# A four-layer transformer and a fifth block on one core: new orders around the sliding-window attention, and mask and maximum in one VectorE instruction

## The reference

```python
scores = jnp.einsum('bnqkgd,bnskd->bnkgqs', qb, kk) * (hd ** -0.5)      # hd = 64, window 128
scores = jnp.where(mask[None, :, None, None], scores, -jnp.inf)          # causal band of 128 keys
sink_col = broadcast(sinks)                                              # one logit for each head
probs = jax.nn.softmax(jnp.concatenate([scores, sink_col], axis=-1), axis=-1)[..., :-1]
out = jnp.einsum('bnkgqs,bnskd->bnqkgd', probs, vv)
```

## Time and profile before

| | |
|---|---|
| median of three runs | 1664.19 us |
| profiled execution | 1669.89 us, of which the span of the core is 1668.1 |
| TensorE matmul / DVE / ScalarE / GpSimd busy | 96% / 73% / 47% / 5% |
| mean granted clock of TensorE | 0.98 |
| first layer's attention, after its first two units | 54.3 to 142.2 us |
| the same in the fourth layer | 1051.0 to 1120.7 us |

### The profile page before, as it was taken

The page is one execution under the profiler, slowest core; times in us unless marked ns, Lnnn a source line. Parts: engine busy times, 40 slices in busy tenths (PEclk is TensorE's granted clock), DMA queues, the critical chain, the costliest instruction groups (busy, mean ns, idle before and its releaser), DMA issues.

```text
span 1668.1 us, 30815 instructions
## 1 busy us (share of the span) xinstructions
PE 1593.7 (96%) x12553; PEld 1504.7 (90%) x12553; DVE 1211.3 (73%) x1619; ACT 792.0 (47%) x1042; POOL 91.1 (5%) x105
## 2 busy tenths in 40 slices
PE   2969999999999999999999999989999999999998
PEld 1848999999989999988899999869999988889998
DVE  6887877778368777765487777958777777676665
ACT  2444433356265334454453334555433467654543
POOL 0131000001000000001100000120000012300000
PEclk8988999999899999999999999999999999999999
DMA  9755787855246888562359785525978745345550
GB/s 391 301 200 204 314 316 293 310 193 199 90 180 250 332 305 317 209 247 101 141 211 362 295 307 221 215 79 201 368 293 319 264 159 166 117 155 194 184 176 26
DMA packets 54219, 383.75 MB, mean 230 GB/s; under 512 B 6256, under 2 KB 6512, under 8 KB 8448
## 3 DMA queue, kind: packets, MB, share of 16 engines
q1 hardware_dynamic: 50400, 363.75, 58.2%
q0 software_dynamic: 3744, 18.94, 3.1%
HBM read 378.47 MB, written 4.19 MB: 229 GB/s over the span
## 4 chain that ended last, share of the span: by engine, by line
PE 85%; DVE 8%; DMA 4%; ACT 1%; issue 1%; POOL 0%; SPq 0%; DVEq 0%; ACTq 0%
PE PS L1855 70%; PE PS L1876 5%; DVE wlo L1329 2%; PE PS L1997 2%; DMA adar<-ada 2%; DMA CST<-cst_in 1%; DVE adar L1347 1%; PE PS L1922 1%; PE PS L1886 1%; DMA raw<-ada 1%; DVE RB L1503 1%; PE PS L2044 1%; DVE SCR L1497 1%; PE PS L1896 1%; PE PS L1976 1%
## 5 line engine op out<-in xcount | busy, mean ns | idle before, releaser
L1855 PE MATMUL PS<-hhi,whi 128*128 128x256 f32 x2496 | 718.7, 288 | 21.8 <-DVE hlo L1537 18.4
L1329 DVE TENSOR_TENSOR wlo<-raw,whi 128x2048 fp32r<-128x2048 f32 x234 | 537.0, 2295 | 247.2 <-ACT whi L931 246.8
L1855 PE MATMUL PS<-hlo,whi 128*128 128x256 f32 x2496 | 711.7, 285 | 0.0
L1855 PE MATMUL PS<-hhi,wlo 128*128 128x256 f32 x2496 | 711.5, 285 | 0.0
L931 ACT ACTIVATE whi<-raw 128x2048 fp32r<-128x2048 f32 x234 | 446.9, 1911 | 483.9 <-PE PS L1855 478.9
L1855 PEld LDWEIGHTS PS<-hhi,whi 128*128 128x128 f32 x2496 | 484.6, 194 | 32.1 <-DVE hlo L1537 20.4
L1855 PEld LDWEIGHTS PS<-hlo,whi 128*128 128x128 f32 x2496 | 484.8, 194 | 1.3 <-issue 1.2
L1855 PEld LDWEIGHTS PS<-hhi,wlo 128*128 128x128 f32 x2496 | 484.6, 194 | 0.0
L1347 DVE CUSTOM_DVE_ANT_0 adar<-adar,CB 128x1024 f32<-128x1024 f32 x232 | 277.0, 1234 | 12.3 <-DMA adar<-ada 12.1
L1855 PE MATMUL PS<-ahi,whi 128*128 128x256 f32 x968 | 274.5, 284 | 1.1 <-DVE alo L1805 1.1
L1855 PE MATMUL PS<-alo,whi 128*128 128x256 f32 x968 | 273.9, 283 | 0.0
(11 more groups left out here) (235 smaller groups left out, 1407.8 us busy)
## 6 DMA issues: line engine op xcount, KB each, us to landing
raw<-weights SPq DMA_DIRECT2D x234, 1024.0 KB, 6.4
adar<-ada SPq DMA_DIRECT2D x104, 1024.0 KB, 6.0
adar<-ada POOLq DMA_DIRECT2D x12, 1024.0 KB, 7.3
raw<-ada SPq DMA_DIRECT2D x4, 1024.0 KB, 15.1
bias_rows<-acc POOLq DMA_DIRECT2D x12, 256.0 KB, 2.9
adar<-bias_rows POOLq DMA_DIRECT2D x8, 256.0 KB, 3.1
CST<-cst_in SPq DMA_DIRECT2D x1, 1128.0 KB, 22.7
CB<-c_in SPq DMA_DIRECT2D x2, 512.0 KB, 4.4
```

Source lines behind the costliest of these rows:

```text
L1329: v.tensor_tensor(wlo[:, u % CV, :], raw[:, u % RAW, :], whi[:, u % CV, :].bitcast(F32), ALU.subtract).then_inc(lo_done, 1)
L1855: m = pe.matmul(o, w(a), h(b), start=first and k_ == 0, stop=last and k_ == 2, skip_group_check=True)
```

## The change

Three things change. First, `mask_max` of swa and fox. Each head and query tile is one fused instruction: (scores + mask) x -1/8 written out, and the minimum of it, starting from the negated sink (or from 1e30 in fox), accumulated. The stored values are the negated scores, so the exponentials scale by -1. In fox the exponentials wait for `s_masked`, since there is no second signal.

```diff
-                        mask = bc(cst("masks", n, 0 if kind == "fox" else 2 * P), 2)
+                        mask = cst("masks", n, 0 if kind == "fox" else 2 * P)
+                        for k, (a, b) in enumerate(segments(kind)):
+                            for h in range(2):
+                                sink = 16 * kinds[:l].count("swa") + 2 * p + h
+                                least = nsink[:, sink:sink + 1] if kind == "swa" else -NEG
+                                mx = v.tensor_tensor_reduce(out=t[:, h, a:b], in0=PS[:, 4 + h, a:b], in1=mask[:, a:b], scale=-(HD ** -0.5), scalar=least,
+                                                            op0=ALU.add, op1=ALU.min, accum_out=nm[:, 2 * k + h:2 * k + h + 1])
+                        mx.then_inc(s_masked, 1)
+                        if kind == "swa":
+                            v.wait_ge(s_masked, J + 1)
+                            k = 16 * kinds[:l].count("swa") + 2 * p
+                            mx = v.tensor_tensor(two(sk), two(nm), bc(par("sinks", 2, k), 2), ALU.add)
+                            mx.then_inc(st_max, 1)
+                        return
...
-                        e = act.activation(x, x, ACT.Exp, bias=nm[:, k:k + 1], accum_out=den[:, k:k + 1])
+                        e = act.activation(x, x, ACT.Exp, scale=1.0 if kind == "b2" else -1.0, bias=nm[:, k:k + 1], accum_out=den[:, k:k + 1])
```

(`max` is `mask_max`, `mlo` is `mixed_lo`.) Product 9's second half and its sum move to the third output unit. ScalarE's list, for both swa layers:

```diff
+                    if l:
+                        hi(u0 + 3)
+                        hi(u0 + 4)
                     rope_read(0)
                     rope_read(1)
-                    hi(u0 + 3)
-                    hi(u0 + 4)
+                    if l == 0:
+                        hi(u0 + 3)
+                        hi(u0 + 4)
+                    hi(u0 + 5)
                     unit_read(2, V[:, :, 0:UC])
...
                 for i in range(OUT_UNITS):
-                    if l == 0 and i == 0:
+                    if l == 0 and i == 2:
+                        ada_sum(9, 1, 1)
                         ada_read(9)
```

Third, GpSimd's list in the first layer. `first_ada` issues one half now; before, the normalising of pairs 1, 3, 5 and 7 was each followed by both halves of products 6, 7, 8 and 9:

```diff
                 if l == 0:
-                    first_ada(4)
-                    first_ada(5)
+                    first_ada(4, 0)
+                    first_ada(4, 1)
+                    first_ada(5, 0)
+                    first_ada(5, 1)
+                    first_ada(6, 0)
...
-                        if l == 0 and p in (1, 3, 5, 7):
-                            first_ada(6 + p // 2)
+                        if l == 0 and p == 1:
+                            first_ada(6, 1)
+                        if l == 0 and p == 3:
+                            first_ada(7, 0)
+                            first_ada(7, 1)
+                        if l == 0 and p == 4:
+                            first_ada(8, 0)
...
```

More of the change, by code:

```diff
@@ L1022, in exps @@
                 def exps(p):
-                    act.wait_ge(st_max, pos0[l] + p + 1)
+                    if kind == "fox":
+                        act.wait_ge(s_masked, pos0[l] + p + 1)
+                    else:
+                        act.wait_ge(st_max, pos0[l] + p + 1 - PAIRS * ("fox" in kinds[:l]))
                     t = prob_tile(kind, p)
@@ new lines, in _ @@
+                        lo(u0 + 4)
+                        lo(u0 + 5)
+                        mask_max(1)
+                        recips(0)
+                        rope(3)
+                        recips(1)
+                        lo(u0 + 6)
+                        mask_max(2)
+                        ada_sum(5, 1, 1)
+                        recips(2)
+                        rope(4)
+                        mask_max(3)
+                        lo(u0 + 7)
+                        mask_max(4)
@@ L1591, in _ @@
+                        mixed_lo(0)
+                        recips(3)
                         ada_read(5)
-                    mask_max(3)
-                    mixed_lo(0)
-                    if l == 0:
                         ada_sum(6, 0, 0)
-                    mask_max(4)
-                    recips(3)
-                    rope(5)
-                    if l == 0:
+                        rope(5)
+                        mixed_lo(1)
+                        mask_max(5)
                         ada_sum(6, 1, 0)
-                    mask_max(5)
@@ L1613, in _ @@
+                        recips(5)
                         ada_sum(7, 1, 1)
-                    mask_max(7)
-                    recips(6)
-                    if l == 0:
+                        mask_max(7)
+                        recips(6)
                         ada_read(7)
                         ada_sum(8, 0, 0)
-                    mixed_lo(3)
-                    recips(7)
-                    mixed_lo(4)
-                    if l == 0:
+                        recips(7)
+                        mixed_lo(4)
@@ L1623, in _ @@
                         ada_sum(8, 1, 0)
+                        mixed_lo(5)
+                        mixed_lo(6)
                         ada_read(8)
-                    mixed_lo(5)
-                    if l == 0:
+                        ada_sum(9, 0, 1)
+                        mixed_lo(7)
                         lo(u0 + 8)
-                        ada_sum(9, 0, 1)
-                    mixed_lo(6)
-                    if l == 0:
-                        ada_sum(9, 1, 1)
-                    mixed_lo(7)
+                    else:
+                        lo(u0 + 3)
+                        lo(u0 + 4)
+                        rope(0)
+                        rope(1)
+                        lo(u0 + 5)
+                        mask_max(0)
+                        ada_all(mixer_ada(l)[0])
+                        recips(0)
+                        mask_max(1)
+                        rope(3)
+                        recips(1)
+                        ada_read(mixer_ada(l)[0])
+                        lo(u0 + 6)
+                        mask_max(2)
+                        rope(4)
+                        recips(2)
+                        mask_max(3)
+                        lo(u0 + 7)
+                        mixed_lo(0)
+                        mask_max(4)
+                        recips(3)
+                        rope(5)
+                        mixed_lo(1)
+                        recips(4)
+                        mask_max(5)
+                        mixed_lo(2)
+                        mask_max(6)
+                        recips(5)
+                        mixed_lo(3)
+                        mask_max(7)
+                        recips(6)
+                        mixed_lo(4)
+                        recips(7)
+                        mixed_lo(5)
+                        lo(u0 + 8)
+                        mixed_lo(6)
+                        mixed_lo(7)
```

93 lines of the change are left out of this document (35 added, 58 removed).

## The result

The changed kernel takes 1656.12 us (median of four runs, 1655.81 to 1656.83). The kernel before took 1665.43 beside it (four runs, 1663.74 to 1668.35). The ratio is 0.9934, with a 95% interval of 0.992 to 0.9948. So it is faster by 9.3 us, where the forecast said 21.3 and its range ended at 1655. The profiled executions are 14.1 us apart, 1669.89 and 1655.81 us (spans 1668.1 and 1654.0).

The account below looks back on a forecast made before the run. TensorE is busy 1593.7 of 1668.1 us, so only its waits and lower clock could be won; DVE bounds the first layer, order the fourth. 12.7 + 7.8 + 0.8 = 21.3 us; 1664.2 - 21.3 = 1642.9, range 1633 to 1655.

Parts of the forecast that it names:

- The new pass: Mask pass of a swa pair on DVE: 1.4 us instead of 2.3, saving 7.4 us a swa layer.
- First layer: First layer's attention: `mixed_lo(7)` ends 14.3 us earlier, 1.6 given back behind it, so 12.7 us gained; ends 6 and 27.
- middle term: First layer up to `mixed_lo(7)`: DVE loses 12.0 us of work, its waits fall from 6.8 to 4.5, 14.3 us earlier.
- Third layer: Third layer's one TensorE wait of 1.9 us, behind scores(7), shrinks with the shorter pass: 0.8 us gained, bounds 0 and 1.9.
- Fourth layer: Fourth layer's attention: 7.7 us of waits and 1.2 of clock go, 1.1 come back: 7.8 us gained, ends 4 and 8.9.
- a new wait comes: Fourth layer: ScalarE rounds two units before the two rope reads, so TensorE waits 0.8 us for the first.
- The orders alone give about 10: In two rivals, with a dear pass only the new order works: 6 + 4 + 0.2 us in first, fourth and third layers.
- The offset: Whole kernel: the runs' median stands 5.7 us below the profiled execution, a difference taken as it is.
- Slower: Rival, chance 0.04: `s_masked` signalled by the last of four instructions delays scores; at 3.5 us a pass, 8 slower: 1672.
- The pass is dear: Rival, chance 0.12: the mask pass takes 2.0 to 2.3 us, only the order works, about 10 us gained: 1654.
- The first layer stays bound by its weights: Rival, chance 0.17: GpSimd's weight halves land late, the first layer gives 7, the sum is 15.6: 1648.6.
- three signs of being wrong: Pass over 2 us; DVE waiting over 7 us for `adar`; or waits gone but granted clock at 0.5 as long as now.

Follow-up runs that it names:

- e9: e2 with, in the first layer alone, VectorE's rounding of the second MLP unit moved behind the last two X updates and their sums of squares: 1645.82 us, ratio 0.987.
- e11: The kernel of e9 once more, on another chip: 1649.7 us, ratio 0.9891 to the kernel before.
- e1: Changed kernel with the fourth layer's modulation product put back right behind the rounding lo(u0+2): 1647.32 us, ratio 0.9888 to the kernel before.
- e2: Changed kernel with SyncE's load of the second condition vector, and its wait, moved behind the first two output weight units: 1646.18 us, ratio 0.987.
- e4: Changed kernel in all its new orders, with the old three instructions for mask and maximum: 1667.18 us, ratio 0.9998 to the kernel before.
- e5: e2 with ScalarE's first two rope reads of the fourth layer put ahead of the roundings hi(u0+3) and hi(u0+4): 1650.24 us, ratio 0.9889.
- e6: e2 with VectorE's rounding lo(u0+8) of the fourth layer moved from beside GpSimd's last normalisation to behind mixed_lo(4): 1647.77 us, ratio 0.989.

## Why the prediction was wrong, point by point

- **The new pass: right within its bounds.** 1.4 us forecast, within 1.3 to 2.0; measured 1.55, so it saves 6.0 us a layer and not 7.4. The sign that the fused rows read 0.2 to 0.25 and 0.35 us failed: they read 0.35 and 0.48, with steps of 0.27 and 0.40. The Trainium skill (VectorE: DVE Perf Modes, the section on the TRN2 errata) gave an estimate of 1.5, and that was nearer than mine.
- **First layer: 1.7 us too large, and its middle term right by luck.** `mixed_lo(7)` ended at 126.45 us, forecast 126.4. But DVE waited 0.8 us before that point instead of the 4.5 taken, and its busy time fell by 8.0 us instead of 12.0: two errors of some 4 us that cancel. That weight halves would land late was wrong; that GpSimd's normalising would lengthen DVE's rows beside it was in no term. The last X update ended at 143.4 (forecast 126.4 + 16.8 = 143.2). The term that shows in the total is what is given back, 1.6 us, measured 3.3 from `mixed_lo(7)` to the MLP mark (30.4 us before, 33.7 now). It stopped at the last X update, and behind it TensorE ran the sums of squares and its warm-up products on the lower clock, after it had waited 2.2 us. e9 got 3.6 us there, and e11 2.3, by moving one subtraction.
- **Third layer: right**, 1.1 us of wait, 0.9 us gained, of which 0.8 are TensorE's idle time.
- **Fourth layer: the step that failed.** The forecast said "a new wait comes" and counted one, the rope reads at 0.8 us. That one came, at 0.8. It took the loop of mask, exponentials and `mixed_lo` as the whole of the order. The moved modulation product is not named in that step at all, so it was costed at nothing, and SyncE's load that waits for it was not followed. e1 and e2 show that this queue took 7.7 us. Without it the layer gains 7.0 us (293.7 to 286.7) against the forecast 7.8, so the rest of the step held to 0.8 us, though e2 still has 2.8 us of waits (1.6 of them for GpSimd, which had no term of its own) where the forecast left 1.1. Its bounds, 4 to 8.9, held only edits of DVE and ScalarE, and so the whole range ended 1 us too early.
- **"The orders alone give about 10"** (in two rivals): they give nothing in e4. In the fourth layer it rested on the same missing queue. In the first it said 6 and e4 shows 3.3, for which no run shows the reason. The pass was the surer half.
- **The offset.** The sum was made against a profiled execution with the second layer at 342.4 us, and 5.7 us were taken off to reach the median of three runs. The changed kernel's own profiled execution and median differ by 0.3 us. The lapse of the clock stood in the first trace; that it differs from execution to execution, one execution could not show. And three runs were few: in the four groups the kernel before has medians of 1667.2 to 1668.5 us over 11 to 17 runs that spread over 6 to 9.3 us, so 0.2% was too fine a measure.
- **The miss added up.** 1656.1 is 13.2 us above 1642.9. The offset makes 6.0 of it. The other 7.2 are 8.5 in the fourth layer, 1.7 in the first and 1.6 in the last stretch, less 4.5 in the second and 0.1 in the third. Without the queue's 7.7 us the median would have been near 1648 (an estimate from e1 and e2), inside the range.
- **Slips in the working.** 69.7 - 7.8 is 61.9 and not 61.5. In "Slower", (3.5 - 2.3) x 16 less 10 is 9.2 us and not 8.
- **The rivals.** None was what happened. "The pass is dear" gives 1654, near the measured 1656, for a reason that is false: the pass is cheap. "The first layer stays bound by its weights" is refuted, since DVE waits for none of them between 55.69 us and the end of `mixed_lo(7)`. None of the three signs of being wrong came true either: all of them looked at the pass, DVE's waits and the clock, and none at a DMA queue.

The Trainium skill (GPSIMD Engine Reference, Key points) says that GpSimd and a DVE instruction with two SBUF inputs contend. The trace agrees: 1.04 us alone, 3.09 beside the subtraction of two SBUF tiles.

## What to carry to other kernels

When an instruction moves on one engine, look up who waits for its semaphore, on the DMA queues too, and then read what stands behind that wait in the queue: here a load issued at 1054.30 us and first read at 1126.98 held up weights for which ScalarE stood idle. A load with a late condition goes behind those whose slots are already free. Where two edits lie on the same busy engine, measure each alone, since the gain of the whole can be that of one half, with the other half's gain lost elsewhere.

## What was not expected of the hardware

- TensorE's granted clock falls in the second layer though it is 20.00 us busy of 20.00, in more than two forms (0.70 over twenty microseconds in the kernel before, 0.91 in the changed one, and e4's between them). Between two profiles this made up to 6 us, and the runs of one kernel spread by up to 9 us. What decides the form stays open.
- A wait of 2.2 us of TensorE was followed by 1.5 us of lost clock in the next 14 instructions (2.91 + 2.46 against 1.97 + 1.89 us). In e5 a wait of 2.1 us is followed by a granted clock of 0.57 over four microseconds, and in e6 one of 1.9 us by 0.59.
- A GpSimd multiplication of 512 columns takes three times as long beside a DVE subtraction, 3.09 against 1.04 us, while the subtraction itself goes from 2.29 to only 2.61. The subtraction runs from 1095.55 to 1098.16 us, and the multiplication beside it ends at 1099.06, about the length of one alone behind the end of the subtraction. The other way round, the first step of `rope` on DVE goes from 0.68 to 1.52 us beside such a multiplication.
